# Per-head norms in four column strips, and two projection outputs moved behind the first output projection: one decoder step on one core

## The chip, the cores and the metric

The kernel runs on one core of a Trainium2 chip. The metric is the device time of one execution in microseconds (us). Before the change the median of three runs is 1661.73 us (1660.33 to 1661.95).

## What is computed

Two decoder layers on 576 tokens of width 1024: 512 prompt tokens and 64 sampled tokens (8 sequences of 8). A layer is, cut to what matters here:

```
h = rms_norm(x, g_mix_pre);  proj = h @ w_in          # q, f, i, g of 4 recurrent heads; q, k, v of 8 attention heads
rec  = gated_linear_recurrence(...)                   # 4 heads, width 128
rec  = rms_norm_per_head(rec, g_rec_out) * silu(g)
attn = dilated window attention (three patterns mixed)# 8 heads, width 64
attn = rms_norm_per_head(attn, g_attn_out)
x = x + rms_norm(concat(rec, attn) @ w_out, g_mix_post)
h = rms_norm(x, g_mlp_pre);  u = relu(h @ w_up) ** 2
x = x + rms_norm(u @ w_down, g_mlp_post)
```

## The kernel before

Activations stay in SBUF with channels on partitions and tokens along the free dimension. Tokens are split in two halves: half 0 has 320 tokens (64 sampled, 256 prompt), half 1 has 256. Every weight block of 1024x128 is loaded once or twice, split on ScalarE and VectorE into a high part (`w_high`, line 702) and a rest (`w_rest`, line 1275), and used in three matmuls per 128 rows (rest by high, high by rest, high by high): 24 matmuls make one **output**, a PSUM tile of 128 channels by 320 or 256 tokens (`gemm`, lines 952 and 955). A ring of four weight slots and two PSUM banks lies between outputs.

The order of the work is written out by hand. `phases()` (line 51) lists the outputs: `IA`, the input projection of half 0 (28 outputs); `IB`, that of half 1, cut in two; between its parts `OA`, the output projection of half 0 (8 outputs); then `U0A` and so on, the MLP. In `IB` come the blocks F, Q and G (4 outputs each), I (4), QA, K and V (4 each). Everything else is a **step** hung behind one output by `steps_at()` (line 104): on each engine, the step's instructions follow those of its output, in program order. Steps that matter here:

- `r_sum`, `r_spr`: the norm of the recurrent heads. TensorE sums squares (line 1128: the squares are the stationary operand, one column of ones moves, one matmul for each head and tile of 128 tokens; the sum stands with tokens on partitions), ScalarE takes the root (lines 829, 830), VectorE the reciprocal (lines 1491, 1492, 8 columns), and TensorE spreads it over 128 partitions (line 1139, by the identity), whence VectorE scales (1500, 1505), ScalarE and GpSimd split the product (840, 660) for the output projection.
- `a_sum`, `a_spr`: the same for the attention heads (lines 1241 and 1253 on TensorE, 1572 to 1581 on VectorE, 891 and 892 on ScalarE, then 1589, 897, 667). The softmax denominators enter as `den2`.
- `norm_sum 1` (line 983): the sum of squares of the output projection's result over channels, with `post 1`, which adds the scaled result to x and squares x (lines 1313, 1316, 710, 1288), and then `norm_sum 2` and `pre 2`, which make the MLP's input (1328, 1333). On VectorE the reciprocal is line 1298.
- `upd 1` (line 1059, VectorE 1468), the update of the recurrent state for half 1; `out 1` (lines 1075 and 1078), its output; `lev`, the levels of the recurrence (line 1019); `s_sel`, `s_pt`, `s_sc`, `s_pv`, `s_div`, the attention of the sampled tokens.

TensorE instructions of type f32 appear twice in the trace (two passes); fp32r ones once. In the trace all of them are written as f32.

## Time and profile before

| | |
|---|---|
| median of 3 runs | 1661.73 us |
| the profiled execution, its own time | 1659.98 us |
| its span | 1658.1 us |
| mean granted TensorE clock | 0.989 of full |
| TensorE busy | 1600.8 us, 97% |
| VectorE, ScalarE, GpSimd busy | 966.7, 832.4, 197.2 us |

The time outside the span is 1.9 us. Matmuls are pipelined: what a block of them costs on TensorE is the distance from its start to the start of the next, and not the sum of its durations.

### The profile page before, as it was taken

The page shows a single profiled execution, that of the slowest core. Times are in us where ns is not written, and L with a number is a line of the kernel's source. Part 1 is how long each engine was busy: PE and PEld are TensorE (multiplying, and loading weights), DVE is VectorE, ACT ScalarE, POOL GpSimd, SP SyncE. Part 2 cuts the span into 40 slices and gives each one's busy share as a digit, 9 for nine tenths or more (in the row PEclk, how much of TensorE's full clock was granted, in tenths as well). Part 3 has the DMA queues.
Part 4 walks back from the last instruction along what each step waited for, and adds up shares of the span by engine and source line. Part 5 has one row for each costly group of instructions (what it writes and reads, how often), then busy time and mean ns, then how long its engine had stood idle before and what let it go on. Part 6 is the DMA issues. An engine that isn't in the chain of part 4 may idle for free.

```text
span 1658.1 us, 30046 instructions
## 1 busy us (share of the span) xinstructions
PE 1600.8 (97%) x12176; PEld 1524.4 (92%) x12176; DVE 966.7 (58%) x1597; ACT 832.4 (50%) x1482; POOL 197.2 (12%) x225
## 2 busy tenths in 40 slices
PE   5999999989999999999999999999999999999996
PEld 5998779988999999999899987899889999999995
DVE  6753646594456655335987445467744575553475
ACT  6426443447464755334664363434664566551552
POOL 3220103120000100000213100142100010000011
PEclk9999999999999999999999999999999999999998
DMA  5544553334355555334454454343534545552443
GB/s 197 190 143 158 199 194 109 121 132 141 106 162 153 165 180 185 120 111 146 152 153 123 152 208 174 127 137 94 172 105 138 165 151 170 187 181 90 128 153 108
DMA packets 83188, 247.82 MB, mean 149 GB/s; under 512 B 8771, under 2 KB 26435, under 8 KB 82924
## 3 DMA queue, kind: packets, MB, share of 16 engines
q1 hardware_dynamic: 83052, 245.90, 46.7%
q8 instruction: 98, 1.61, 0.4%
q14 instruction: 38, 0.31, 0.1%
HBM read 234.05 MB, written 14.44 MB: 150 GB/s over the span
## 4 chain that ended last, share of the span: by engine, by line
PE 87%; DVE 8%; ACT 2%; DMA 1%; issue 1%; SPq 0%; POOLq 0%; POOL 0%; DVEq 0%; ACTq 0%
PE ps L955 66%; PE ps L952 6%; PE ps L1019 3%; DVE w_rest L1275 2%; PE ps L1155 1%; PE ps L1168 1%; PE ps L1183 1%; PE ps L1198 1%; DVE reg L1313 1%; DVE square_sum L1288 1%; DMA kc<-kcT 1%; DVE norm_every L1298 1%; PE ps L1221 1%; PE ps L1108 1%; PE ps L1253 1%
## 5 line engine op out<-in xcount | busy, mean ns | idle before, releaser
L955 PE MATMUL ps<-h_high,w_rest 128*128 128x320 f32 (+1 forms) x1920 | 580.7, 302 | 7.2 <-DVE h_rest L1333 6.2
L955 PE MATMUL ps<-h_high,w_high 128*128 128x320 f32 (+1 forms) x1920 | 569.3, 297 | 0.0
L955 PE MATMUL ps<-h_rest,w_high 128*128 128x320 f32 (+1 forms) x1920 | 569.3, 297 | 0.0
L702 ACT ACTIVATE w_high<-w_raw 128x1024 fp32r<-128x1024 f32 x384 | 402.1, 1052 | 233.3 <-PE ps L955 233.0
L1275 DVE TENSOR_TENSOR w_rest<-w_raw,w_high 128x1024 fp32r<-128x1024 f32 x380 | 480.8, 1269 | 64.6 <-ACT w_high L702 64.3
L955 PEld LDWEIGHTS ps<-h_high,w_rest 128*128 128x128 f32 x1920 | 365.2, 190 | 24.5 <-issue 20.1
L955 PEld LDWEIGHTS ps<-h_rest,w_high 128*128 128x128 f32 x1920 | 365.5, 190 | 0.4
L955 PEld LDWEIGHTS ps<-h_high,w_high 128*128 128x128 f32 x1920 | 365.3, 190 | 0.0
L955 PE MATMUL ps<-u_high,w_rest 128*128 128x320 f32 (+1 forms) x1024 | 305.3, 298 | 3.9 <-DVE u_rest L1375 3.2
L955 PE MATMUL ps<-u_high,w_high 128*128 128x320 f32 (+1 forms) x1024 | 303.1, 296 | 0.0
L955 PE MATMUL ps<-u_rest,w_high 128*128 128x320 f32 (+1 forms) x1024 | 303.1, 296 | 0.0
L955 PEld LDWEIGHTS ps<-u_high,w_rest 128*128 128x128 f32 x1024 | 194.4, 190 | 6.5 <-DVE u_rest L1375 3.8
L955 PEld LDWEIGHTS ps<-u_rest,w_high 128*128 128x128 f32 x1024 | 194.4, 190 | 0.1
L955 PEld LDWEIGHTS ps<-u_high,w_high 128*128 128x128 f32 x1024 | 194.4, 190 | 0.0
L1375 DVE TENSOR_TENSOR u_rest<-tmp,u_high 128x256 fp32r<-128x256 f32 (+1 forms) x128 | 59.1, 462 | 130.1 <-ACT u_high L795 130.1
L1357 DVE TENSOR_TENSOR reg<-reg,ps 128x320 f32<-128x320 f32 (+1 forms) x96 | 43.5, 453 | 142.2 <-PE ps L955 142.2
L676 POOL TENSOR_TENSOR x<-x,reg 128x320 f32<-128x320 f32 (+1 forms) x32 | 39.8, 1243 | 717.1 <-DVE reg L1313 717.1
L762 ACT ACTIVATE tmp<-ps 128x256 f32<-128x256 f32 (+1 forms) x128 | 52.4, 409 | 120.5 <-PE ps L955 120.5
L952 PE MATMUL ps<-w_rest,h_high 128*128 128x256 f32 (+1 forms) x320 | 94.8, 296 | 0.0
L952 PE MATMUL ps<-w_high,h_rest 128*128 128x256 f32 (+1 forms) x320 | 90.9, 284 | 0.0
L952 PE MATMUL ps<-w_high,h_high 128*128 128x256 f32 (+1 forms) x320 | 90.9, 284 | 0.0
L1437 DVE COPY_PREDICATED sc<-masks,ps 128x256 f32<-128x256 uint8 x56 | 29.6, 529 | 79.4 <-PE ps L1019 69.3
(176 smaller groups left out, 1763.2 us busy)
## 6 DMA issues: line engine op xcount, KB each, us to landing
w_raw<-w SPq DMA_DIRECT2D x384, 512.0 KB, 3.5
kc<-kcT SPq DMA_DIRECT2D x16, 512.0 KB, 6.8
vc<-vc SPq DMA_DIRECT2D x16, 512.0 KB, 6.6
s_in<-s SPq DMA_DIRECT2D x8, 512.0 KB, 5.7
ss<-s_in SPq DMA_DIRECT2D x8, 512.0 KB, 5.7
bias<-rel_scratch SPq DMA_DIRECT2D x8, 512.0 KB, 4.4
rel_scratch<-rel_row SPq DMA_DIRECT2D x1, 2560.0 KB, 12.8
bias<-rel_scratch SPq DMA_DIRECT2D x8, 256.0 KB, 5.3
```

The costliest lines, as they stand in the source:

```text
L676: V.tensor_tensor(x[:, c, cols], x[:, c, cols], acc[h][:, c, :], ALU.add).then_inc(S["x_odd"], 1)
L702: A.activation(whi[:, v % RING], raw[:, v % RING], ACT.Copy).then_inc(S["w_hi"], 1)
L762: A.activation(tmp[:, s, 0:n], src, ACT.Relu).then_inc(S["ev_a"], 1)
L952: last = pe.matmul(ps[0:rows, bank, 0:256].rearrange("p (s n) -> p s n", s=2), xt[:, c, t0:t0 + rows], wt[:, slot:slot + 2, c, :], **flags)
L955: last = pe.matmul(ps[:, bank, 0:n], wt[:, slot, c, :], xt[:, c, :], **flags)
L1019: last = pe.matmul(to(ps[:, bank, o0:o0 + n]), kb[h][:, a, pro(h, c)], right(qq[h][:, a, pro(h, c)]), start=True, stop=True)
L1108: pe.matmul(ps[:, 2, a * TS + c:a * TS + c + TB], s_in[a][:, b, :], qq[0][:, a, c:c + TB], start=False, stop=(b == NB - 1), skip_group_che ...
L1155: last = pe.matmul(ps[:, 5 + s, b0 * P:(b0 + nb) * P], qa[h][r, j, pro(h, u % 2)], src[r, j, c0:c0 + nb * P], start=True, stop=True)
L1275: V.tensor_tensor(wlo[:, v % RING], raw[:, v % RING], whi[:, v % RING].bitcast(F32), ALU.subtract).then_inc(S["w_lo_d"], 1)
L1357: V.tensor_tensor(dst, dst, src, ALU.add).then_inc(S["ev_d"], 1)
L1375: V.tensor_tensor(ul[o.h][:, o.k, :], tmp[:, 2 + k % 2, 0:n], uh[o.h][:, o.k, :].bitcast(F32), ALU.subtract).then_inc(S["u_set"], 1)
L1437: V.copy_predicated(out=right(sc[h][:, heads[g], :].rearrange("p a t -> p (a t)"), 4), mask=masks[:, lv - 1, :].rearrange("p (n s) -> p n ...
```

## The change

- `IB` is cut after 16 units instead of 18 (18 outputs instead of 20), so `OA` starts two outputs earlier and 10 outputs of 256 tokens, instead of 8, follow it (QA 2 and 3 now among them).
- The first half's `r_sum` and its two `r_spr` hang one output earlier (7, 8, 9). The levels of half 1 start one output earlier, with two of them at the first, and their place in `OA` stays.
- Behind `OA`, `upd 1` and `norm_sum 1` hang at the first output instead of the second, `post 1` follows from there; `norm_sum 2` stays at the fifth output, `out 1` moves from the fourth to the sixth; `pre 2` starts at the sixth as before, with one of its five parts there instead of two. `r_sum` and `r_spr` of half 1 stay in front of the last outputs of `IB`.
- The per-head sums are made with the squares as the moving operand. Each head (or pair of attention heads) writes its own 32 PSUM partitions; the sum stands as a row of tokens. The denominators are added by eight small matmuls into the same place. One root and one reciprocal run over 320 (256) columns of all 128 partitions (`head_norm`), and one matmul for each head or pair, with one or two rows of `head_norm` moving, spreads it. `den2` for the attention norm is computed by a step of its own (`a_sq` on VectorE).

```diff
-IB_CUT = 20
+IB_CUT = 18
...
-    cut = 18
+    cut = 16
...
-    put("IB", 8, "r_sum", 0)
-    put("IB", 9, "r_spr", 0, 0)
-    put("IB", 10, "r_spr", 0, 1)
+    put("IB", 7, "r_sum", 0)
+    put("IB", 8, "r_spr", 0, 0)
+    put("IB", 9, "r_spr", 0, 1)
...
-            i = 11 + 2 * lv + g
+            i = 10 + max(0, 2 * lv + g - 1)
             put(*(("IB", i) if i < IB_CUT else ("OA", i - IB_CUT)), "lev", 1, lv, g)
     put("OA", 7, "k_t", 1)
-    put("IB", 21, "upd", 1)
-    put("IB", 21, "norm_sum", 1, 0)
+    put("IB", 18, "upd", 1)
+    put("IB", 18, "norm_sum", 1, 0)
     put("U0A", 1, "v_store", 1)
     for p in range(6):
-        put("IB", 21 + p // 2, "post", 1, 0, p)
+        put("IB", 18 + (p + 1) // 2, "post", 1, 0, p)
     put("IB", 23, "out", 1)
     put("IB", 24, "bias_in", 1, 0)
     put("IB", 24, "bias_in", 1, 1)
-    put("IB", 24, "norm_sum", 2, 0)
+    put("IB", 22, "norm_sum", 2, 0)
     for p in range(5):
-        put("IB", 25 + p // 2, "pre", 2, 0, p)
+        put("IB", 23 + (p + 1) // 2, "pre", 2, 0, p)
...
-    half = np.kron(np.eye(2), np.ones((DH, DH))).astype(np.float32)
     row = np.arange(P)
+    sums = (row[:, None] // DH == np.arange(32)[None] % 2)
+    spread = (row[:, None] % 32 == np.arange(P)[None] // DH)
     seq_of_tok = (row % TS // TB)[:, None] == np.arange(NB)[None]
     head_of_row = ((row % 64) // TB)[:, None] == np.arange(HA)[None]
     tok_of_row = (row // 64 * TB + row % TB)[:, None] == np.arange(2 * TB)[None]
-    cst = np.concatenate([eye, half, seq_of_tok, head_of_row, tok_of_row], 1).astype(np.float32)
+    cst = np.concatenate([eye, spread, seq_of_tok, head_of_row, tok_of_row, sums], 1).astype(np.float32)
...
-    den2 = place("den2", [P, 3 * HA])
-    root = place("root", [P, 3 * HA])
-    inv = place("inv", [P, 3 * HA])
-    r_root = place("r_root", [P, 3 * HR])
-    r_inv = place("r_inv", [P, 3 * HR])
+    den2 = place("den2", [P, 2 * HA])
+    rn = place("head_norm", [P, WIDE[0]])
...
-    half_ones = cst[:, P:2 * P]
+    head_spread = cst[:, P:2 * P]
...
+    head_sum = cst[:, 288:320]
...
             def r_sum(l, h):
+                n = WIDE[h]
                 act.wait_ge(S["r_ms"], 2 * l + h + 1)
-                if h == 0:
-                    A.activation(r_root[0:TS, 8:12], ps[0:TS, 2, 8:12], ACT.Sqrt, bias=eps[0:TS], scale=1.0 / P)
-                A.activation(r_root[:, 0:8], ps[:, 2, 0:8], ACT.Sqrt, bias=eps[:], scale=1.0 / P).then_inc(S["r_root"], 1)
+                if l or h:
+                    act.wait_ge(S["a_spr"], 8 * l + 4 * h)
+                A.activation(rn[:, 0:n], ps[:, 2, 0:n], ACT.Sqrt, bias=eps[:], scale=1.0 / P).then_inc(S["r_root"], 1)
...
             def a_sum(l, h):
-                act.wait_ge(S["a_sum"], 2 * l + h + 1)
+                act.wait_ge(S["a_ms"], 2 * l + h + 1)
+                act.wait_ge(S["r_spr"], 8 * l + 4 * h + 4)
                 if h == 0:
-                    A.activation(root[0:TS, 16:24], den2[0:TS, 16:24], ACT.Sqrt, bias=eps[0:TS], scale=1.0 / DH)
-                A.activation(root[:, 0:16], den2[:, 0:16], ACT.Sqrt, scale=1.0 / DH).then_inc(S["a_root"], 1)
+                    A.activation(rn[:, 0:TS], ps[:, 2, 0:TS], ACT.Sqrt, bias=eps[:], scale=1.0 / DH)
+                A.activation(rn[:, pro(h)], ps[:, 2, pro(h)], ACT.Sqrt, scale=1.0 / DH).then_inc(S["a_root"], 1)
...
-                for t, (t0, rows) in enumerate(TILES[h]):
-                    for a in range(HR):
-                        o0 = 4 * t + a
-                        last = pe.matmul(ps[0:rows, 2, o0:o0 + 1], o_sq[h][:, a, t0:t0 + rows], ones[:, 0:1],
-                                         start=True, stop=True)
+                for a in range(HR):
+                    last = pe.matmul(ps[32 * a:32 * a + 32, 2, 0:WIDE[h]], ones[:, 0:32], o_sq[h][:, a, :], start=True, stop=True)
                 last.then_inc(S["r_ms"], 1)
...
             def r_spr(l, h, g):
                 pe.wait_ge(S["r_inv"], 2 * l + h + 1)
+                take(3, 4)
                 for i in range(2):
                     a = 2 * g + i
-                    take(3 + i)
-                    for t, (t0, rows) in enumerate(TILES[h]):
-                        last = pe.matmul(ps[:, 3 + i, t0:t0 + rows],
-                                         r_inv[0:rows, 4 * t + a:4 * t + a + 1].broadcast_to([rows, P]),
-                                         ident[0:rows, 0:rows], start=True, stop=True)
-                    last.then_inc(S["r_spr"], 1)
+                    pe.matmul(ps[:, 3 + i, 0:WIDE[h]], ones[32 * a:32 * a + 1, :], rn[32 * a:32 * a + 1, 0:WIDE[h]],
+                              start=True, stop=True).then_inc(S["r_spr"], 1)
...
             def a_sum(l, h):
                 pe.wait_ge(S["a_sq"], 2 * l + h + 1)
+                pe.wait_ge(S["a_den"], 2 * l + h + 1)
                 take(2)
-                for t, (t0, rows) in enumerate(TILES[h]):
+                for j in range(HP):
+                    pe.matmul(ps[32 * j:32 * j + 32, 2, 0:WIDE[h]], head_sum, a_sq[h][:, j, :], start=True, stop=False,
+                              skip_group_check=True)
+                for c in range(2):
                     for j in range(HP):
-                        o0 = 8 * t + 2 * j
-                        last = pe.matmul(ps[0:rows, 2, o0:o0 + 2], a_sq[h][:, j, t0:t0 + rows], half_ones[:, 0:P:DH],
-                                         start=True, stop=True)
+                        c0 = HA * c + 2 * j
+                        last = pe.matmul(ps[32 * j:32 * j + 2, 2, pro(h, c)], den2[:, c0:c0 + 2], ident,
+                                         start=False, stop=(c == 1), skip_group_check=True)
                 last.then_inc(S["a_ms"], 1)
-                held[2] = (S["a_sum"], 2 * l + h + 1)
+                held[2] = (S["a_root"], 2 * l + h + 1)
 
             def a_spr(l, h, g):
                 pe.wait_ge(S["a_inv"], 2 * l + h + 1)
+                take(5, 6)
                 for i in range(2):
-                    take(5 + i)
-                    for t, (t0, rows) in enumerate(TILES[h]):
-                        for s in range(2):
-                            c = 8 * t + 2 * (2 * g + i) + s
-                            last = pe.matmul(ps[DH * s:DH * s + DH, 5 + i, t0:t0 + rows],
-                                             inv[0:rows, c:c + 1].broadcast_to([rows, DH]), ident[0:rows, 0:rows],
-                                             start=True, stop=True)
-                    last.then_inc(S["a_spr"], 1)
+                    j = 2 * g + i
+                    r = slice(32 * j, 32 * j + 2)
+                    pe.matmul(ps[:, 5 + i, 0:WIDE[h]], head_spread[r, :], rn[r, 0:WIDE[h]], start=True, stop=True)\
+                        .then_inc(S["a_spr"], 1)
...
                 dve.wait_ge(S["r_root"], 2 * l + h + 1)
-                if h == 0:
-                    V.reciprocal(r_inv[0:TS, 8:12], r_root[0:TS, 8:12])
-                V.reciprocal(r_inv[:, 0:8], r_root[:, 0:8]).then_inc(S["r_inv"], 1)
+                V.reciprocal(rn[:, 0:n], rn[:, 0:n]).then_inc(S["r_inv"], 1)
...
+            def a_sq_(l, h):
+                dve.wait_ge(S["p_exp"], unit(l, h, 7) + 1)
+                if l or h:
+                    dve.wait_ge(S["a_ms"], 2 * l + h)
+                V.scalar_tensor_tensor(den2[:], den[:], DH * EPS, den[:], ALU.mult, ALU.mult).then_inc(S["a_den"], 1)
+
             def a_sum(l, h):
-                dve.wait_ge(S["p_exp"], unit(l, h, 7) + 1)
-                own(V.scalar_tensor_tensor(den2[:, 0:16], den[:], DH * EPS, den[:], ALU.mult, ALU.mult))
-                dve.wait_ge(S["a_ms"], 2 * l + h + 1)
-                if h == 0:
-                    V.tensor_copy(den2[0:TS, 16:24], ps[0:TS, 2, 16:24])
-                own.wait()
-                V.tensor_tensor(den2[:, 0:16], den2[:, 0:16], ps[:, 2, 0:16], ALU.add).then_inc(S["a_sum"], 1)
+                n = WIDE[h]
                 dve.wait_ge(S["a_root"], 2 * l + h + 1)
-                if h == 0:
-                    V.reciprocal(inv[0:TS, 16:24], root[0:TS, 16:24])
-                V.reciprocal(inv[:, 0:16], root[:, 0:16]).then_inc(S["a_inv"], 1)
+                V.reciprocal(rn[:, 0:n], rn[:, 0:n]).then_inc(S["a_inv"], 1)
```

How the instructions stand, at the places that the prediction speaks of. TensorE, first half's recurrent norm sum: before, behind output 8 of `IB`, ahead of the sampled tokens' value product (`vc`):

```order
L955 MATMUL ps<-h_high_59,w_high 128x256
L1128 MATMUL ps<-ones,reg_55 128x1 x8
L1128 MATMUL ps<-ones,reg_55 64x1 x4
L1221 MATMUL ps<-vc_123,probs_st 64x512
L1221 MATMUL ps<-vc_124,probs_st 64x512
```

and in the changed kernel, behind output 7, ahead of the sampled tokens' selection, transposes and scores (`mo`, `probs_s`, `kc`):

```order
L956 MATMUL ps<-h_high_59,w_high 128x256
L1127 MATMUL ps<-reg_55,ones 32x320 x4
L1226 MATMUL ps<-cst,mo_125 128x16 x4
L1203 MATMUL ps<-cst,probs_s 128x128 x2
L1204 MATMUL ps<-cst,probs_s 64x128
L1193 MATMUL ps<-kc_118,qbig 64x264
```

Twelve narrow matmuls became four of 320 columns, and stand one output earlier.

VectorE behind `OA` (from the state update of half 1 to the middle of `post 1`), before:

```order
L1468 SCALAR_TENSOR_TENSOR states<-states,f_tot_1_78,ps 128x128 x8
L1298 RECIPROCAL norm_every<-norm_every 128x320
L1313 SCALAR_TENSOR_TENSOR reg_55<-reg_55,prm,norm_every 128x320 x2
L1316 TENSOR_TENSOR x<-x,reg_55 128x320
L1313 SCALAR_TENSOR_TENSOR reg_55<-reg_55,prm,norm_every 128x320 x2
L1316 TENSOR_TENSOR x<-x,reg_55 128x320
L1275 TENSOR_TENSOR w_rest<-w_raw,w_high 128x1024
```

and in the changed kernel:

```order
L1464 SCALAR_TENSOR_TENSOR states<-states,f_tot_1_78,ps 128x128 x8
L1294 RECIPROCAL norm_every<-norm_every 128x320
L1309 SCALAR_TENSOR_TENSOR reg_55<-reg_55,prm,norm_every 128x320 x2
L1312 TENSOR_TENSOR x<-x,reg_55 128x320
L1271 TENSOR_TENSOR w_rest<-w_raw,w_high 128x1024
L1309 SCALAR_TENSOR_TENSOR reg_55<-reg_55,prm,norm_every 128x320 x2
L1312 TENSOR_TENSOR x<-x,reg_55 128x320
```

The chain starts one output earlier, and one more `w_rest` (three instead of two) stands inside it.

## Rows read from the trace of the kernel before

**Rows 1.** The page's busy times: us (share of the span) xinstructions.
```profile
PE 1600.8 (97%) x12176; PEld 1524.4 (92%) x12176; DVE 966.7 (58%) x1597; ACT 832.4 (50%) x1482; POOL 197.2 (12%) x225
```
**Rows 2.** Waits on PE: for whom, us in total, times, longest us.
```profile
PE ps L983 <- DVE square_sum L1288: 22.4, 4, 10.9
...
PE ps L1168 <- ACT prob L848: 3.6, 3, 1.6
```
**Rows 3.** The chain in time, half 0's norms: start us, us, what.
```profile
229.38 2.18 PE ps L1128 x23
...
237.51 1.81 PE ps L1139 x12
...
259.77 2.24 PE ps L1241 x24
...
275.39 1.70 PE ps L1253 x24
```
**Rows 4.** The chain in time, half 1's attention norm.
```profile
436.50 1.68 PE ps L1241 x16
...
445.32 1.02 PE ps L1253 x16
```
**Rows 5.** The timeline of PE, half 1's recurrent norm: start us, us, engine, line.
```profile
355.08 1.84 PE L1128 MATMUL ps<-ones,reg 128*128 128x1 f32 x16
356.78 0.36 PE L952 MATMUL ps<-w_rest,h_high 128*128 128x256 f32 x1
...
362.61 1.05 PE L1139 MATMUL ps<-cst,r_inv 128*128 128x128 f32 x8
363.42 0.39 PE L955 MATMUL ps<-h_high,w_rest 128*128 128x320 f32 x1
```
**Rows 6.** The timeline of PE and PEld, two column strips of 64.
```profile
245.29 1.94 PE L1221 MATMUL ps<-vc,probs_st 128*64 128x512 f32 x8
247.16 1.12 PE L1223 MATMUL ps<-va_tok,probs_st 64*128 64x512 f32 x2
...
245.29 0.20 PEld L1221 LDWEIGHTS ps<-vc,probs_st 128*64 128x64 f32 x4
```
**Rows 7.** The timeline of PE, two row strips of 64.
```profile
392.04 1.13 PE L1155 MATMUL ps<-key,reg 64*128 64x256 f32 x8
393.10 0.41 PE L955 MATMUL ps<-h_high,w_rest 128*128 128x320 f32 x1
```
**Rows 8.** The timeline of PE, a norm sum over the whole array.
```profile
332.08 0.70 PE L983 MATMUL ps<-square_sum,ones 128*128 128x320 f32 x2
...
332.74 0.28 PE L955 MATMUL ps<-h_rest,w_high 128*128 128x256 f32 x1
332.86 0.28 PE L955 MATMUL ps<-h_high,w_high 128*128 128x256 f32 x1
```
**Rows 9.** Groups by form: xcount, busy us, mean ns, idle before.
```profile
L1298 DVE RECIPROCAL norm_every<-norm_every 128x320 f32<-128x320 f32 x8 | 17.2, 2152 | 6.2 <-ACT norm_every L725 6.2
...
L829 ACT ACT_TABLE_LOAD x2 | 2.6, 1283 | 0.0
```
**Rows 10.** The timeline of PE behind `OA`: the output step, then the wait.
```profile
338.37 0.39 PE L1075 MATMUL ps<-sc,v_tok 128*128 128x128 f32 x2
...
341.86 0.36 PE L952 MATMUL ps<-w_rest,h_high 128*128 128x256 f32 x1
...
350.11 1.44 PE L983 MATMUL ps<-square_sum,ones 128*128 128x320 f32 x2 [5.14 <-DVE square_sum L1288]
```
**Rows 11.** The timeline of DVE, start and end of the chain behind `OA`.
```profile
333.96 2.15 DVE L1298 RECIPROCAL norm_every<-norm_every 128x320 f32<-128x320 f32 x1
...
347.79 2.27 DVE L1288 TENSOR_TENSOR square_sum<-square_sum,squares 128x320 f32<-128x320 f32 x4
```
**Rows 12.** A stretch: from:to, us, PE busy, granted clock, DMA share, GB/s.
```profile
350.00:354.00 4.00, 3.89 (x17) 0.58 0.60 202
```
**Rows 13.** The timeline of POOL: the last split ahead of `OA`.
```profile
279.53 2.61 POOL L667 TENSOR_TENSOR h_rest<-att_sq,h_high 128x640 fp32r<-128x640 f32 x1 [2.85 <-ACT h_high L897]
```

More of the change, by code:

```diff
@@ L342, in build @@
     tmp = place("tmp", [P, 4, WIDE[0]])
-    cst = place("cst", [P, 288])
+    cst = place("cst", [P, 320])
     ones = place("ones", [P, P])
@@ L408, in build @@
              "ss_done", "ss_max", "sp_exp", "sp_norm", "sp_t", "spt_there", "spv_done", "mo_set", "sel_done", "so_there",
-             "a_sq", "a_ms", "a_sum", "a_root", "a_inv", "a_spr", "a_scaled", "a_hi", "a_lo",
+             "a_sq", "a_den", "a_ms", "a_root", "a_inv", "a_spr", "a_scaled", "a_hi", "a_lo",
              "sq", "ssq", "n_ms", "n_root", "n_inv", "nap", "x_even", "x_odd", "h_hi", "h_even", "h_odd",
@@ L1568, in s_pv @@
                                 head_mask.unsqueeze(2).broadcast_to([P, HA, DH]), ALU.mult).then_inc(S["mo_set"], 1)
-            def a_sum(l, h):
-                dve.wait_ge(S["p_exp"], unit(l, h, 7) + 1)
-                own(V.scalar_tensor_tensor(den2[:, 0:16], den[:], DH * EPS, den[:], ALU.mult, ALU.mult))
-                dve.wait_ge(S["a_ms"], 2 * l + h + 1)
-                if h == 0:
-                    V.tensor_copy(den2[0:TS, 16:24], ps[0:TS, 2, 16:24])
-                own.wait()
-                V.tensor_tensor(den2[:, 0:16], den2[:, 0:16], ps[:, 2, 0:16], ALU.add).then_inc(S["a_sum"], 1)
+            def a_sq_(l, h):
[3 more added lines that the diff above has]
+                V.scalar_tensor_tensor(den2[:], den[:], DH * EPS, den[:], ALU.mult, ALU.mult).then_inc(S["a_den"], 1)
+            def a_sum(l, h):
+                n = WIDE[h]
                 dve.wait_ge(S["a_root"], 2 * l + h + 1)
-                if h == 0:
-                    V.reciprocal(inv[0:TS, 16:24], root[0:TS, 16:24])
-                V.reciprocal(inv[:, 0:16], root[:, 0:16]).then_inc(S["a_inv"], 1)
+                V.reciprocal(rn[:, 0:n], rn[:, 0:n]).then_inc(S["a_inv"], 1)
             def a_spr(l, h, g):
@@ L1603, in _ @@
                      "s_upd": s_upd, "r_sum": r_sum, "r_spr": r_spr, "q_big": q_big, "sc": sc_, "s_sc": s_sc, "s_div": s_div,
-                     "s_pv": s_pv, "a_sum": a_sum, "a_spr": a_spr}
+                     "s_pv": s_pv, "a_sq": a_sq_, "a_sum": a_sum, "a_spr": a_spr}
             late = []
```

## Prediction

> **What bounds the kernel now.** First the page's busy times: TensorE is busy for 97% of the span, VectorE for 58%, ScalarE for 50% [rows 1]. So TensorE's own time counts nearly everywhere, and beside it only the places where it waits. Second, its waits: the norm sums of line 983 lead with 22.4 us, of which 10.9 lie at the start of the program; the others are few [rows 2]. Third, the timeline behind `OA`: TensorE reaches the second norm sum after the output that starts at 341.86, and that sum starts only at 350.11, after 5.14 us of waiting for VectorE's last `square_sum` [rows 10]. VectorE works on this chain from the reciprocal at 333.96 to 350.06 with hardly a gap [rows 11]. After the wait the granted clock averages 0.58 for 4 us, so most of the stretch ran at 1.2 GHz instead of 2.4 [rows 12]. The same stands in the second layer. Fourth, what the per-head norms cost TensorE, as starts of blocks, since these blocks stand in stretches where it never idles [rows 3 to 5].
>
> **The norms, removed.** Per layer, half 0: 2.18 us for the recurrent sum, 1.81 for each of two spreads, 2.24 for the attention sum, 1.70 for each of two spreads: 2.18 + 3.62 + 2.24 + 3.40 = 11.44 [rows 3]. Half 1: 1.70 (356.78 less 355.08), twice 0.81 (363.42 less 362.61), 1.68, twice 1.02: 7.04 [rows 4, 5]. All of it is TensorE time, 18.48 us a layer.
>
> **The norms, added.** No matmul with 32 columns or one row stands in this trace, so the price is built from neighbours. A full-array pass over 320 columns: the norm sum and one main matmul take 332.74 - 332.08 = 0.66 us, the main one 0.12 (332.86 - 332.74), which leaves 0.54 for two passes, 0.27 each [rows 8]; 256 columns by proportion 0.215, 128 columns 0.11, 512 columns 0.43. Two column strips of 64: eight passes of 512 columns take 247.16 - 245.29 = 1.87 us, where one after another they would take 3.5; four rounds of 0.43 are 1.73, which leaves 0.14 for entering and leaving the mode [rows 6]. Two row strips: eight passes of 256 columns in 1.06 us, four rounds of 0.215 are 0.86, overhead 0.20 [rows 7]. So strips of two run side by side, in both directions. I take it that four column strips do too, because nothing in rows 6 ties the pairing to the number two; the other end is priced below as a rival.
> - Recurrent sum: four strips, two passes: 0.54 + 0.14 = 0.68; half 1 0.43 + 0.14 = 0.57.
> - Each spread, recurrent or attention: two row strips, two passes, into two banks: 0.54 + 0.20 = 0.74; half 1 0.63.
> - Attention sum: as the recurrent one, and then 16 passes of 128 columns for the denominators. If only the columns count, four rounds of 0.11, 0.43; if each pays its weight load as the narrow blocks do now (2.18 us for 23, 0.09 each [rows 3]), 1.5. I take 0.9, between them, since the strips' loads partly overlap. 1.58; half 1 1.47.
>
> Half 0: 0.68 + 4 x 0.74 + 1.58 = 5.22; half 1: 0.57 + 4 x 0.63 + 1.47 = 4.56. Saved per layer 6.22 + 2.48 = 8.7, in both layers **17.4 us**. The Trainium skill (TensorE: Matmul & The Clock Gate, section "Measured speedup vs the span model") gives less than the ideal for strips, 3.07 times for four row strips. By it an 8-pass sum (2.16 us in line) would take 0.70 instead of 0.54, and four of them a layer would cost 1.1 us more in all over both layers.
>
> **Off TensorE.** The reciprocal grows from 8 or 16 columns to 320, 2.15 us [rows 9], four times a layer (half 1 a little less), about +7 us a layer on VectorE. It costs nothing where the spread comes late enough. The tightest is half 0's recurrent norm: between sum and first spread stand selection, transposes and scores, roughly 3 us, and one output of 24 x 0.12 = 2.9; the way back is a table load on ScalarE (1.28 [rows 9]), a root (I estimate 0.5) and the reciprocal (2.15), behind an output's eviction and weight split of another 1.5, so 5.4. Covered by a few tenths; if not, TensorE waits as long as the rest. With this norm's sum in front, the scores also meet their key load later, which hides a few tenths of waiting. Zero for both.
>
> `OA` now starts one output after the last attention spread instead of three. Today from that spread's start at 275.39 [rows 3] to the end of GpSimd's split at 282.14 [rows 13] pass 6.8 us. The changed order gives it the spread (0.74), one output (2.9), two level steps of 8 short passes (8 x 0.09 = 0.7 each) and three quarters of the first 320-token output (24 x 0.12 x 320/256 x 3/4 = 2.7): 7.7 us. The cover holds by 0.9 us; zero.
>
> **The moves behind `OA`.** The chain starts one output (2.9 us) earlier, counted from the end of `OA`. Inside, it takes on one more weight split, about 1.2 us, to 17.3 instead of 16.1 (350.06 - 333.96 [rows 11]); with the state update the sum is ready 2.3 to 2.7 us earlier. But TensorE arrives earlier too: the output step of 341.86 - 338.37 = 3.5 us [rows 10] now stands behind the sum, not ahead of it. It also meets about 1 us for an eviction that waits on ScalarE behind the squares of `post 1`. The wait is then 5.9 us in all instead of 5.14, and the clock falls as before. Against this, `pre 2` is done well before `U0A`, because two outputs and the output step stand in between; VectorE, which came out of `pre 2` late and pushed the first softmax (1.6 us of waiting for `prob` in a layer [rows 2]), is free, and I keep 0.4 of that wait. Net -0.5 a layer, **-1.0 us**. The two outputs themselves cost the same where they are.
>
> **Sum.** -17.4 - 1.0 = -18.4 on the profiled execution's 1659.98: 1641.6. The median of the runs shown is 1.75 above that execution, so 1643.3.
>
> **Rivals.** (Within 0.2%, 3.3 us, a measurement of this kernel can hardly tell a change.)
> 1. *Four strips run two at a time.* For: only pairs are seen [rows 6, 7]. Then each sum has twice the rounds: +0.54 and +0.43 for either norm, and 0.4 for each denominator block: 2.7 a layer, 5.5 in all, 1648.8.
> 2. *The norm behind `OA` does not come earlier, but loses its cover.* The change says that the chain moves ahead by an output; if VectorE or ScalarE is what it waits for (the last squares, splits or the state update), the wait grows by an output, 2.9 us, and the half-speed stretch by up to 3.4 us, worth 1.7: 4.6 a layer, 1652.5. For: VectorE has no gap in rows 11. Against: the chain's head, the state update, follows TensorE at once, and TensorE gets there an output earlier. A spread that waits for the wide reciprocal costs the same kind of sum and I count it here.
> 3. *Slower: no two strips share the array.* Place: the eight sums and sixteen spreads. Price: recurrent sums 2.30 and 1.86, spreads 1.28 and 1.06, attention sums 4.06 and 3.62, so half 0 11.5 and half 1 9.7 against 11.44 and 7.04: +2.7 a layer, less 1.0 for the moves, +4.4: 1666. It decides as soon as the blocks of a layer exceed 18.5 + 2.1 us. Against: rows 6 and 7, where passes overlap in pairs.
> 4. *Weight loads of column strips are not hidden.* All strips use the same 128 rows. 64 loads a layer of about 0.1 us, less the 0.9 already counted, would cost 5.5 a layer, 11 in all, beyond what is counted: 1654. Against: four loads are issued within 0.20 us of the block's start, under matmuls that run on [rows 6]. The Trainium skill (TensorE: Matmul & The Clock Gate, section "The mechanism") says that loads overlap running matmuls only when their row group differs, which speaks for this rival; the trace disagrees for two strips.
> 5. *The wait behind `OA` no longer drops the clock*, and denominators cost only their columns: -1.7 and -0.9 a layer, 1638.
>
> **Chances.** Forecast 0.52, rival 1 0.16, rival 2 0.15, rival 3 0.05, rival 4 0.05, rival 5 0.07. The range goes from rival 5, 1638, to 1656, which takes in rivals 1, 2 and 4 and rival 1 with part of 2; outside are rival 3, rivals 1 and 2 in full, and what I have not thought of. Faster by over 0.2% (below 1658.4): all but rival 3 and some mixtures, 0.88; same 0.07; slower 0.05.
>
> **What would show it.** In the changed trace: the recurrent sum's block at 0.6 to 0.8 us with four starts a few ns apart (rival 1: pairs; rival 3: starts 0.27 apart); spreads at 0.6 to 0.8; the attention sum at 1.2 to 2.2; TensorE at nearly the same share of a span about 18 us shorter; the wait ahead of the second norm sum at 4.5 to 6.5 us with a half-speed stretch behind it, the wait for `prob` under 1 us; no new wait at the first output of `OA` or ahead of the first spread. I am wrong if the blocks shrink and the span does not, or if the wait behind `OA` is above 8 us.

## The result, and the profile after

The changed kernel takes 1645.82 us (median of four runs, 1642.87 to 1646.43), beside 1661.84 for the kernel before (four runs). The ratio is 0.9893, interval 0.9866 to 0.992: 1.1% faster (the two medians alone give 0.9904; one of the four runs before took 1667.86). Predicted were 1643.3, range 1638 to 1656. The profiled execution took 1645.60 us against 1659.98 before, 14.4 less. Two executions of the experiments below (1762.88 us of the kernel before and 1781.06 of moves_only, at granted clocks of 0.84 and 0.83) are in none of the ratios and ranges.

The page's busy times after, to hold against [rows 1]:

```profile
PE 1584.7 (96%) x11968; PEld 1499.6 (91%) x11968; DVE 978.3 (60%) x1587; ACT 831.7 (51%) x1478; POOL 193.9 (12%) x225
```

TensorE lost 16.1 us of busy time, VectorE gained 11.6, and the span shrank by 14.3: the time went down with TensorE's.

The blocks of the first layer, half 0, in the timeline of PE (start us, us, engine, line, operation; [rows 3] have them before). First the recurrent sum, then a recurrent spread, the attention sum with its denominators, an attention spread, each with the instruction behind it:

```profile
221.65 0.28 PE L956 MATMUL ps<-h_high,w_high 128*128 128x256 f32 x1
221.85 0.74 PE L1127 MATMUL ps<-reg,ones 128*32 128x320 f32 x8
222.53 0.28 PE L1226 MATMUL ps<-cst,mo 128*128 128x16 f32 x1
...
228.89 0.81 PE L1136 MATMUL ps<-head_norm,ones 1*128 1x320 f32 x4
229.62 0.65 PE L1216 MATMUL ps<-vc,probs_st 128*64 128x512 f32 x2
...
257.15 0.74 PE L1235 MATMUL ps<-att_sq,cst 128*32 128x320 f32 x8
257.72 0.62 PE L1240 MATMUL ps<-cst,den 128*2 128x128 f32 x16
258.27 0.99 PE L1020 MATMUL ps<-reg 128*128 128x64 f32 x7
...
265.99 0.81 PE L1251 MATMUL ps<-head_norm,cst 2*128 2x320 f32 x4
266.73 0.43 PE L1020 MATMUL ps<-reg 128*128 128x64 f32 x2
```

The recurrent sum costs 222.53 - 221.85 = 0.68 us instead of 2.18, a spread 0.73 instead of 1.81, the attention sum 1.12 instead of 2.24, its spread 0.74 instead of 1.70. Half 0's norms come to 0.68 + 2 x 0.73 + 1.12 + 2 x 0.74 = 4.74; half 1's, read in the same way, are 0.57, twice 0.63, 1.01 and twice 0.63, 4.1. That is 8.85 a layer against 18.48: **9.6 us saved in each layer, 19.2 in all**. The costs before are pieces of the chain, from end to end; the chain after gives the same as the starts here (0.68, 0.74, 1.12, 0.74). Read from start to start, the blocks before are a little longer (1.90 for a recurrent spread, 2.33 for the attention sum), and the saving would be some 9.9 a layer.

The weight loads of the recurrent sum, in the timeline of PEld:

```profile
221.85 0.16 PEld L1127 LDWEIGHTS ps<-reg,ones 128*32 128x32 f32 x8
```

All eight loads are done within 0.16 us of the block's start, under the first matmuls.

The waits on PE (for whom, us in total, times, longest; [rows 2] before):

```profile
PE ps L984 <- DVE square_sum L1284: 22.0, 4, 10.8
PE ps L956 <- DVE h_rest L1329: 5.8, 2, 5.3
...
PE ps L956 <- ACT key L780: 3.4, 2, 1.7
...
PE ps L1163 <- ACT prob L848: 1.1, 3, 0.4
```

Behind `OA`, the timeline of PE; [rows 10] before:

```profile
327.12 0.36 PE L956 MATMUL ps<-h_high,w_rest 128*128 128x256 f32 x1 [1.72 <-ACT key L780]
...
335.11 1.44 PE L984 MATMUL ps<-square_sum,ones 128*128 128x320 f32 x2 [4.88 <-DVE square_sum L1284]
```

Two stretches (from:to, us, then PE, PEld, DVE, ACT, POOL busy, the granted clock, DMA share, GB/s; [rows 12] before):

```profile
334.40:341.20 6.80, 6.09 (x25) 5.71 (x26) 5.74 (x7) 2.04 (x4) 0.00 (x0) 0.50 0.54 157
...
221.00:231.00 10.00, 10.00 (x79) 6.82 (x77) 4.84 (x8) 7.46 (x13) 0.00 (x0) 1.00 0.71 247
```

The wait behind `OA` is now 1.72 + 4.88 = 6.6 us instead of 5.14, and the clock stays at 1.2 GHz (0.50) for 6.8 us. In the trace of before that stretch is 3.4 us long in the first layer and 6.8 in the second; after, 6.8 in both, and one more, of 3.4 us at 805 us, that before does not have; before has one of 3.4 at 207 that after does not have. The second stretch above is one of the norm's own: TensorE never idles, at full clock.

**The account of the 14.4 us.** Blocks: -19.2. Waits: norm sums -0.4, `prob` -2.5, `h_rest` -0.4, `key` +3.4, five small ones together +1.5: +1.6. Clock: the half-speed stretches of a whole execution (without the last 15 us, where little is left for TensorE) come to 23.9 us before and 27.3 after; with the waits inside them left out, TensorE worked 20.3 us at half speed before and 25.8 after, and half of that is lost time: +2.8. Sum: -14.8. The clock term describes these two executions; it is not shown to come from the change. A second execution of the changed kernel (after_again, below) has 34.1 us of half-speed stretches, in which TensorE worked 29.7. In the trace of before, the wait of 5.14 us in the first layer has a stretch of 3.4 us behind it, and the shorter one of 4.94 us in the second layer one of 6.8. And the stretch at 805 us stands behind a wait that before has too, at 812.44 us, with the clock at 1.00 around it:

```profile
804.07 0.39 PE L956 MATMUL ps<-u_high,w_rest 128*128 128x256 f32 x1 [2.42 <-DVE u_rest L1371]
812.44 0.39 PE L955 MATMUL ps<-u_high,w_rest 128*128 128x256 f32 x1 [2.42 <-DVE u_rest L1375]
```

### The profile page after: what moved, and what is told of

Same layout as the page of the kernel before. It is cut to its first block, busy times and chain, and to the rows that moved or that the text cites. A ratio compares the mean times of both kernels' runs of the same rounds, so it can differ in the third digit from the quotient of the medians.

```text
span 1643.8 us, 29624 instructions
## 1 busy us (share of the span) xinstructions
PE 1584.7 (96%) x11968; PEld 1499.6 (91%) x11968; DVE 978.3 (60%) x1587; ACT 831.7 (51%) x1478; POOL 193.9 (12%) x225
## 4 chain that ended last, share of the span: by engine, by line
PE 89%; DVE 7%; ACT 2%; issue 1%; DMA 1%; POOL 0%; SPq 0%; POOLq 0%; DVEq 0%; ACTq 0%
PE ps L956 67%; PE ps L953 7%; PE ps L1020 3%; DVE w_rest L1271 2%; PE ps L1150 1%; PE ps L1163 1%; PE ps L1178 1%; PE ps L1193 1%; DVE reg L1309 1%; DVE square_sum L1284 1%; PE ps L1216 1%; DVE norm_every L1294 1%; PE ps L1109 1%; DMA kc<-kcT 1%; PE ps L1218 1%
## 5 line engine op out<-in xcount | busy, mean ns | idle before, releaser
L675 POOL TENSOR_TENSOR x<-x,reg 128x320 f32<-128x320 f32 (+1 forms) x32 | 35.0, 1093 | 718.8 <-DVE reg L1309 718.8
## 6 DMA issues: line engine op xcount, KB each, us to landing
rel_scratch<-rel_row SPq DMA_DIRECT2D x1, 2560.0 KB, 11.6
```

The source lines that it names most:

```text
L675: V.tensor_tensor(x[:, c, cols], x[:, c, cols], acc[h][:, c, :], ALU.add).then_inc(S["x_odd"], 1)
```

## The experiments

Each ran beside the kernel before, in three groups: strips_only, moves_only, out_early and warm; after_again, recip_twice, twice and warm_out; out_early_2, norm_late, norm_late_out and spr_late. In these groups that kernel ranged from 1660.1 to 1670.7, with the granted clock of its executions (0.990 down to 0.982), so kernels are compared by their ratio to it. Of the groups only the second holds the changed kernel itself; a difference of under 0.3% across groups is not told from none, and small effects are read in the trace.

### The norms alone, the moves alone

**strips_only** has the new norms, all steps where they were; **moves_only** the old norms and the new order. Part of the second one's edit, which is all scheduling lines of the change (the first is the rest of it):

```diff
-IB_CUT = 20
+IB_CUT = 18
-    put("IB", 8, "r_sum", 0)
+    put("IB", 7, "r_sum", 0)
...
-    put("IB", 21, "norm_sum", 1, 0)
+    put("IB", 18, "norm_sum", 1, 0)
...
-    put("IB", 24, "norm_sum", 2, 0)
+    put("IB", 22, "norm_sum", 2, 0)
```

> The new norms (strips, one wide root and reciprocal) in the old order of outputs and steps. Theory: the shorter TensorE blocks carry the whole gain, 9.6 us a layer as the changed kernel's trace shows them, and the moves are worth little: 1641 to 1645 us. Rival: the moves carry a part of it, so that this alone gives 1650 us or more. The wait behind OA should be about 5 us in each layer, as before.

Measured: 1651.12 us, ratio 0.9904 (0.988 to 0.9927). In time that is above the 1641 to 1645 expected and in the rival's region; as a ratio it is 1645.9 on the result's 1661.84, and the kernel before was slower in this group than there.

> The old norms in the new order. Theory: the moves gain 1.4 us a layer at the first softmax and lose about 1.5 us a layer at the wait behind OA (1.7 us for an eviction and 4.9 us for the norm sum, against 5.1 us), and up to 1.7 us by a longer stretch at half clock: 1659 to 1664 us. Rival (the prediction's term): a gain of 1 us, or more with the strips taken out: 1657 us or less. If the last attention spread now stands too close to OA, TensorE waits at OA's first output for GpSimd's split.

Measured: 1666.32 us, ratio 1.000 (0.9985 to 1.0015): no gain, as the theory had it, and not the rival's. (In time it is above the 1659 to 1664 expected, as the kernel before is in this group.)

**after_again** is the changed kernel itself, beside the next group.

> The changed kernel as it is, on the chip of the next three. All theories: the same ratio to the kernel before as in the result, 0.989 (0.987 to 0.992). It is the base from which the next three are read. If its half-speed stretches lie elsewhere or are of another number than in the first profile of it, a difference of one such stretch (3.4 us long, 1.7 us of time) between two kernels is chance and no effect of an edit.

Measured: 1645.63 us, ratio 0.9888 (0.9869 to 0.9907). By ratio the norms carry nearly the whole gain. The moves alone give nothing; on top of the new norms they are worth 0.9904 less 0.9888, 0.16% or 2.7 us, but the intervals overlap and the two ran in different groups, so that is no more than the sign of an effect. The medians are 5.5 us apart. The waits of moves_only, behind the same `OA`:

```profile
338.99 0.36 PE L955 MATMUL ps<-h_high,w_rest 128*128 128x256 f32 x1 [1.72 <-ACT key L781]
...
346.96 1.44 PE L983 MATMUL ps<-square_sum,ones 128*128 128x320 f32 x2 [4.87 <-DVE square_sum L1288]
```

They are those of the changed kernel to 0.01 us: the 6.6 us come from the moves, and the norms have no part in them. strips_only keeps one wait of 4.93 us there, but shows a wait for `h_rest` of 1.26 us and one of 0.82 for `prob` at the start of `U0A`, which the moves remove (0.39 us for `prob` is left). Behind these waits its trace has a half-speed stretch of 3.4 us in either layer that the changed kernel does not have; that is where the moves may gain a little once the norms are short.

### Is a block's length on TensorE the kernel's time?

**twice** makes the recurrent sums and all spreads twice into the same place; the result is not changed.

```diff
-                for a in range(HR):
+                for a in (*range(HR), *range(HR)):
...
+                for i in range(2):
+                    a = 2 * g + i
+                    pe.matmul(ps[:, 3 + i, 0:WIDE[h]], ones[32 * a:32 * a + 1, :], rn[32 * a:32 * a + 1, 0:WIDE[h]],
+                              start=True, stop=True)
...
```

> The recurrent heads' sums are made twice into the same place, and each spread, recurrent and attention, is made twice too: per layer two more sums of four column strips and eight more pairs of row strips. Theory (TensorE's time at these places is the kernel's time, and four column strips run side by side): a second sum costs 0.54 us in half 0 and 0.43 in half 1, a second pair of spreads 0.54 and 0.43, so per layer 0.97 for the sums and 4 x 0.54 + 4 x 0.43 = 3.88 for the spreads: 4.85, and 9.7 us in all, 0.6% of the kernel. Rival (the shorter blocks gave time only because waits elsewhere moved): under 4 us. Rival (strips run in pairs once the queue is full): 0.97 more a layer, 11.6 us.

Measured: 1658.87 us (1651.72 to 1660.79), ratio 0.9956 (0.9937 to 0.9974), 13.2 us over the median of after_again, which ran with it. Part of that is the clock: five of the seven executions had 0.983 or 0.984 and took 1658.1 to 1660.8, two had 0.988 and 0.989 and took 1653.4 and 1651.7. At 0.988 after_again took 1644.85, so at the same clock the doubled blocks cost 8.6 us. The timeline of PE:

```profile
223.94 1.28 PE L1127 MATMUL ps<-reg,ones 128*32 128x320 f32 x16
225.15 0.40 PE L1230 MATMUL ps<-cst,mo 128*128 128x16 f32 x2
...
231.51 0.81 PE L1136 MATMUL ps<-head_norm,ones 1*128 1x320 f32 x4
232.15 0.70 PE L1140 MATMUL ps<-head_norm,ones 1*128 1x320 f32 x4
232.78 0.65 PE L1220 MATMUL ps<-vc,probs_st 128*64 128x512 f32 x2
```

A second sum makes the block 1.21 instead of 0.68, +0.53; the second pair of spreads 1.27 instead of 0.73, +0.54. Summed over the trace, the doubled blocks take 9.7 us more, as worked out; the profiled execution lies 13.3 over that of after_again, and the half-speed stretches grow from 34.1 to 41.0 us, worth 3.4 at most. So TensorE's time at these places is the kernel's time, and four strips cost two rounds of 0.27 where a queue of 16 passes stands behind them too. The rival of pairs falls: it asks for 1.08 more for a second sum.

### How wide are the covers?

**recip_twice** puts a second reciprocal of the same width, into a scratch tile, ahead of each of the four of a layer (`rn` is the tile `head_norm`).

```diff
+                V.reciprocal(junk[:, 0:n], rn[:, 0:n])
                 V.reciprocal(rn[:, 0:n], rn[:, 0:n]).then_inc(S["r_inv"], 1)
```

> Ahead of each of the four wide reciprocals of a layer's per-head norms stands a second one of the same width, into a scratch tile. That is about 2.1 us more VectorE work four times a layer, 17 us in all. Theory (the reciprocal is covered by TensorE's work, narrowly for half 0's recurrent norm): behind a reciprocal of 2.15 us there is less than 2.15 us of cover in one or two of the places, so VectorE's new 17 us cost 0 to 5 us, and where they cost, TensorE shows a new wait ahead of the first spread (line 1136) or at OA's first output. Rival (VectorE's time is on the path there already): all of it shows, +10 to +17 us, with waits at every spread.

Measured: 1653.94 us, ratio 0.994 (0.9923 to 0.9957), 8.3 us over after_again: between the two theories, and more than the 0 to 5 expected. First the places of the changed kernel, its DVE timeline:

```profile
225.16 2.15 DVE L1487 RECIPROCAL head_norm<-head_norm 128x320 f32<-128x320 f32 x1 [1.23 <-ACT head_norm L830]
```

It ends at 227.3, and the spread starts at 228.89, when the output ahead of it is done: 1.6 us of cover. Then recip_twice, timeline of PE:

```profile
231.07 0.54 PE L1137 MATMUL ps<-head_norm,ones 1*128 1x320 f32 x2 [0.42 <-DVE head_norm L1489]
...
244.66 0.65 PE L1217 MATMUL ps<-vc,probs_st 128*64 128x512 f32 x2 [1.70 <-ACT probs_st L876]
...
284.88 0.29 PE L1021 MATMUL ps<-reg 128*128 128x64 f32 x1 [0.78 <-issue]
```

The spread itself waits 0.42 us, as 2.1 less 1.6 asks. The rest is paid elsewhere: the sampled tokens' softmax, next in VectorE's queue, makes the value product wait 1.70, and a level step starts 0.78 late with no releaser named, each in both layers. Over the whole trace the waits for `probs_st` are 2.8 us longer than in after_again, those of the level steps 2.1, those for `head_norm` 1.5, and several small ones some 3 together. One reciprocal is free; a second is not, mostly for what is queued behind it.

**spr_late** hangs the second attention spread of half 0 one output later, the last ahead of `OA`.

```diff
-    put("IB", 16, "a_spr", 0, 1)
+    put("IB", 17, "a_spr", 0, 1)
```

> The changed kernel with the second attention spread of half 0 one output later, behind the last output ahead of OA. From the spread to the end of GpSimd's split of its product pass 7 to 8 us, and the prediction gave OA's first output a cover of 7.7 us, 0.9 more than is needed. With one output (2.9 us) of it gone, a new wait of about 2.0 us stands in OA's first output in each layer, 4 us in all (more if a half-speed stretch follows). Rival (the cover was larger than counted, since the last row block is read last): under 1.5 us. Rival (OA was not covered before either, and the split is what it starts on): 5.8 us or more.

Measured: 1646.43 us, ratio 0.9886 (0.9865 to 0.9906), the same as the changed kernel; the 4 us expected did not come, and the first rival (under 1.5 us) did. Its timeline of PE:

```profile
282.74 0.42 PE L956 MATMUL ps<-h_high,w_rest 128*128 128x320 f32 x1 [0.69 <-POOL h_rest L666]
```

And of POOL:

```profile
280.21 2.48 POOL L666 TENSOR_TENSOR h_rest<-att_sq,h_high 128x640 fp32r<-128x640 f32 x1 [1.16 <-ACT h_high L898]
```

`OA`'s first output waits 0.69 us a layer for the split that ends at 282.69. An output of cover (2.9 us) taken away costs 0.7, so 2.2 us were to spare, not 0.9, and the prediction's zero at this place stands.

### What the wait behind OA costs, and where it goes

**out_early** (and again, beside the last group, **out_early_2**) puts the state output of half 1 back ahead of the second norm sum.

```diff
-    put("IB", 23, "out", 1)
+    put("IB", 21, "out", 1)
```

> The changed kernel with out 1 behind output 21 of IB, ahead of the second norm sum, instead of behind output 23. Theory: its 3.5 us of matmuls stand where TensorE waits 1.7 us for an eviction and 4.9 us for the sum, so the two waits fall from 6.6 to about 3.1 us a layer and the stretch at half clock gets shorter: 7 to 12 us less than the changed kernel, 1634 to 1639 us. Rival: ScalarE's four copies of out 1 (2.4 us) delay the squares or the root, and the wait stays: 1643 us or more.

> The same kernel as with out 1 moved alone, on the chip of the next three, as their base: ratio 0.984 to the kernel before (0.982 to 0.9865). It has a wait of 3.3 us left ahead of the second norm sum behind OA, twice.

Measured: 1640.26 us, ratio 0.984 (0.9817 to 0.9864), and 1639.81, 0.9845 (0.9822 to 0.9868): some 0.45% below the changed kernel by ratio, 5.4 us by the medians, 6.9 between the profiled executions (expected were 7 to 12). **warm** leaves the order and fills the wait with 36 matmuls that nobody reads, into bank 5:

```diff
+                if k == 2 and h == 0:
+                    take(5)
+                    for i in range(36):
+                        pe.matmul(ps[:, 5, 0:256], hh[1][:, i % KC, 0:P], hh[1][:, i % KC, :], start=True, stop=True)
```

> The changed kernel with 36 more main-type matmuls of 256 columns (4.3 us at full clock), into a bank that nobody reads, in front of the second norm sum behind OA, where TensorE would wait 4.9 us. It adds work and takes no wait away. Theory: the half-speed stretch behind that wait (6.8 us in both layers) does not come, worth up to 3.4 us a layer: 1639 to 1643 us. Rival: the clock falls for another reason, or it costs nothing because VectorE is behind anyway: 1645 us or more.

Measured: 1642.18 us, ratio 0.9845 (0.9823 to 0.9866). The stretch of 20 us behind `OA` (columns as above), of the changed kernel:

```profile
325.00:345.00 20.00, 13.41 (x87) 12.64 (x86) 17.10 (x23) 9.30 (x17) 2.53 (x3) 0.83 0.40 129
```

Of out_early:

```profile
325.00:345.00 20.00, 16.73 (x127) 16.34 (x126) 17.55 (x24) 11.39 (x22) 3.95 (x4) 0.91 0.40 119
```

Of warm:

```profile
325.00:345.00 20.00, 17.71 (x145) 17.18 (x143) 19.36 (x27) 9.78 (x18) 4.22 (x4) 1.00 0.32 106
```

With the dummies the granted clock stays at 1.00 here, and the sum itself waits 0.57 us. Of the waiting almost nothing is saved: TensorE is idle for 49.4 us of the whole trace instead of 59.1, 9.7 less, and the dummies last 8.7. The two half-speed stretches behind `OA`, 13.6 us long together, are gone; TensorE had worked 12.2 us in them, so 6.1 of time come back. Warm is 0.43% (7 us) below the changed kernel by ratio, 3.6 us by the medians, and the profiled executions differ by 1645.60 - 1642.72 = 2.9 us. This last number is smaller because two stretches of the first layer, at 187 and 207 us, are 13.7 us long in all, where the changed kernel's trace has 3.4. They can't come from the dummies, the first of which runs only later:

```profile
334.66 4.48 PE L985 MATMUL ps<-h_high 128*128 128x256 f32 x36
```

The same 40 us, from 180 to 220, in two executions of the changed kernel, after and after_again:

```profile
180.00:220.00 40.00, 39.17 (x258) 28.35 (x257) 23.77 (x50) 14.85 (x26) 3.10 (x5) 0.96 0.53 181
180.00:220.00 40.00, 40.00 (x245) 27.85 (x245) 21.96 (x45) 14.68 (x26) 3.11 (x5) 0.87 0.49 169
```

The clock of this stretch differs from one execution to the next of one kernel, and in after_again 10.2 us of it are at half speed. out_early shortens the wait to 3.3 us and loses the one for `key`; its stretches behind `OA` are 3.4 us long.

**warm_out** has both, with 20 dummies.

> Two edits at once: the state output of half 1 goes back ahead of the second norm sum behind OA (out 1 at the fourth output of that stretch), and 20 matmuls of 256 columns whose result nobody reads fill what is left of TensorE's wait there. Theory (the wait's price is its length plus a half-speed stretch behind it, 6.8 us long, worth 3.4 us): no half-speed stretch behind OA in either layer, and 4 to 8 us less than the changed kernel, at or below the kernel with out 1 moved alone. Rival (the chip falls to half speed as often, only elsewhere): the stretches appear at other places, and the time is that of out 1 moved alone within 1 us.

Measured: 1642.71 us, ratio 0.9864 (0.9841 to 0.9886), 2.9 us below after_again and no better than out_early; the theory's 4 to 8 us did not come. The rival is right about the place: behind `OA` there is no stretch at half speed, but in either layer one of 3.4 us comes 20 us further on, at 356.2 in the first, behind a wait of 1.6 us for `head_norm` that is new. It is not right about the time, which lies 2.5 us above out_early's, and the new wait is a part of that:

```profile
355.00:360.00 5.00, 4.53 (x19) 4.12 (x20) 4.97 (x8) 1.48 (x2) 0.50 (x1) 0.66 0.51 172
```

**norm_late** moves the second norm sum and `pre 2` one output later; **norm_late_out** does so with `out 1` ahead.

```diff
-    put("IB", 22, "norm_sum", 2, 0)
+    put("IB", 23, "norm_sum", 2, 0)
     for p in range(5):
-        put("IB", 23 + (p + 1) // 2, "pre", 2, 0, p)
+        put("IB", 24 + (p + 1) // 2, "pre", 2, 0, p)
```

> The changed kernel with only the second norm sum behind OA and pre 2 one output later. Theory (length of the wait, then clock): the wait falls from 4.9 to 2 us in either layer; 5.8 us of waiting and some half-speed time go, 5 to 9 us less than the changed kernel, near the kernel with out 1 moved alone. Rival: out 1 now follows right behind the sum, pre 2 comes later, and what is saved comes back ahead of U0A: less than 2 us.

> out 1 moved as before, and the second norm sum behind OA one output later, pre 2 with it. The sum is ready when it was, and TensorE comes to it 2.9 us later, so the wait of 3.3 us falls to some 0.4. Theory (the wait's length and the half-speed stretch behind it are the price): 2.9 us less in either layer and 1.7 to 3.4 less for the stretch, 6 to 11 us below the kernel with out 1 moved alone, if pre 2 is still done in time. Rival (VectorE's chain takes the place of the wait): pre 2 ends 2.9 us later, near the start of U0A, the first softmax or the first half of U0A's output waits for it, and the gain is under 2 us, with waits for prob or h_rest of 1 to 3 us a layer in the list.

Measured: norm_late 1648.14 us, ratio 0.9893 (0.9871 to 0.9916), no gain; norm_late_out 1637.97, ratio 0.9832 (0.981 to 0.9855), 1.8 us under out_early_2, less than the two can tell apart. Both theories (5 to 9 and 6 to 11 us) fail, and both rivals (under 2 us) hold. Neither waits for `square_sum` there any more; norm_late_out waits 2.06 us for `key` and 1.68 for `prob` in its place. The timelines of norm_late show what took its place. PE:

```profile
327.74 0.36 PE L956 MATMUL ps<-h_high,w_rest 128*128 128x256 f32 x1 [1.72 <-ACT key L780]
334.51 0.36 PE L956 MATMUL ps<-h_high,w_rest 128*128 128x256 f32 x1 [3.68 <-ACT key L780]
```

ACT:

```profile
333.03 1.07 ACT L709 ACTIVATE squares<-x 128x320 f32<-128x320 f32 x2 [1.92 <-DVE square_sum L1284]
334.00 0.37 ACT L780 ACTIVATE key<-ps 128x256 f32<-128x256 f32 x1
```

The `key` evictions stand in ScalarE's queue behind the squares of `post 1`, which wait for VectorE. There are two PSUM banks for outputs, so TensorE stops at the next output instead of at the sum: 3.68 us in place of 4.88. And `pre 2` ends later: the wait for `prob` is back at 1.7 us.

## Why the prediction was right, point by point

- *Sum and range.* 18.4 us less were forecast on the profiled execution, 14.4 came. Two errors of opposite sign meet in part: the blocks gave 1.8 us more than counted, waits and clock took 5.4 (+1.6 and +2.8 instead of -1.0). By the medians the miss is only 2.5 us (1645.82 for 1643.3), and the ratio of 0.9889 stands beside 0.9893 and 0.9888. That closeness is luck in part: the forecast added 1.75 us from the profiled execution to the median, and after the change that distance is 0.2; and the ratio of the result's medians is 0.9904.
- *Norms, removed.* 18.48 a layer, half 0 read from pieces of the chain and half 1 in part from starts; all from starts it is some 18.8, a difference of 0.3 a layer. twice shows that time in such blocks is paid in full.
- *Recurrent sum and spreads, added.* 0.68 / 0.57 and 0.74 / 0.63 forecast, 0.68 / 0.57 and 0.73 / 0.63 measured. The price of two strips, rounds plus 0.14 for the mode, carries over to four.
- *Attention sum.* The failed step of the blocks: "I take 0.9, between them" for the 16 denominator passes. The lower end was near: 258.27 - 257.72 = 0.55 from the first of them to the next block, which is what four rounds of 0.11 and some 0.1 for leaving the mode would give, and the whole block took 1.12 instead of 1.58. The upper end had priced a load for each, from narrow blocks that have no strips.
- *Reciprocal.* Covered, by 1.6 us and not "a few tenths". *OA.* Covered, by 2.2 us and not 0.9.
- *Behind OA.* Forecast 5.9 us of waiting, measured 6.6: the 1.72 for `key` was in the text as "about 1 us", the 4.88 as the rest. The wait for `prob` was forecast at 0.4 and is 0.4. The term that the sum did not hold is the clock: "the clock falls as before" was priced at nothing, and between the two profiled executions it is 2.8 us (the first layer's stretch is 6.8 us long instead of 3.4, and another stands at 805 us). Whether the longer waits made it is open: the same kernel's executions differ by as much.
- *The moves,* -1.0 forecast: 1.000 alone, -0.16% on top of the norms, neither told from -1.0. The parts of this term were wrong all the same: the waits that the moves touch grew by 0.5 us in all (+3.4 for `key`, -0.4 for the norm sums, -2.5 for `prob`) instead of falling by 1.0.
- *Rivals.* 1 (pairs) falls by the block of 0.68 and by twice. 3 (no sharing) falls by the same block, for which it asks 2.30. 4 (loads not hidden) falls: eight loads are done in 0.16 us under the matmuls. The Trainium skill (TensorE: Matmul & The Clock Gate, section "The mechanism"), by which loads overlap running matmuls only in another row group, does not hold for column strips in this trace. The Trainium skill (TensorE: Matmul & The Clock Gate, section "Measured speedup vs the span model") gives 3.07 times for four row strips; taken for the whole block, 2.16 us in line, that is an estimate of 0.70. The block of four column strips measured 0.68. The prediction set that 0.70 against its 0.54, which leaves out entering and leaving the strips, so its 1.1 us more was no loss to expect. 2 (the sum behind `OA` gains a wait) was true in size for a part, 1.5 us a layer instead of 4.6. 5 was half true: the denominators cost near their columns (0.55), but the clock still fell.

## What to carry to other kernels

Make the sums over partitions of several heads with the data moving and 32 columns of weights a head: the four share the array, and took 0.68 us here instead of 2.18. Where TensorE waits for a chain on two other engines, look at the queues first: moving the waiting matmul later only helps if the PSUM banks ahead of it are emptied by an engine that the chain does not hold up, and useful work that stands just behind the wait belongs ahead of it (`out 1`, 5 us here). Price a wait of some 5 us at its length and a stretch at half speed behind it (3.4 or 6.8 us long here, worth half of what TensorE works in it). And before you put a change in the half-speed time down to an edit, look at a second execution of the same kernel, and at stretches that lie ahead of the edit.

## What the runs showed of the hardware that I had not expected

- The loads of four column strips over the same 128 rows are all hidden: 0.16 us for eight. The starts of the four strips lie 7 ns apart, and 273 ns pass from the last start of the first round to the first of the second.
- Sixteen accumulating passes with two columns of weights and 128 moving columns take 0.55 us, against 2.24 for 24 narrow ones without strips before [rows 3].
- A filled wait kept the granted clock at 1.00 behind `OA` in warm, but in warm_out a drop came 20 us later behind a wait of 1.6 us. What sets it off there stays open.
- One kernel has 27.3 us of half-speed stretches in one execution and 34.1 in another, at times within 0.5 us. TensorE worked 25.8 us in the first and 29.7 in the second, which is worth 1.9 us; the waits listed are some 1.2 us shorter in the second.
